# Scores before values in the entries of the stick-breaking attention units

## What is computed

```python
def stick_breaking(q, k, v, q_pos, k_pos):
    z = jnp.einsum('bqhd,bkhd->bhqk', q, k, ...) * (HEAD_DIM ** -0.5)
    earlier = k_pos[None, :] < q_pos[:, None]
    log_beta = jax.nn.log_sigmoid(z)
    log_keep = jnp.where(earlier, jax.nn.log_sigmoid(-z), 0.0)
    log_later = lax.cumsum(log_keep, axis=3, reverse=True) - log_keep
    weights = jnp.where(earlier, jnp.exp(log_beta + log_later), 0.0)
    return jnp.einsum('bhqk,bkhd->bqhd', weights.astype(v.dtype), v)
```

## Time and profile before

| what | value |
|---|---|
| median of three runs | 2002.44 us |
| profiled execution, its own time | 2002.01 us |
| its span on the core | 2000.3 us, granted TensorE clock 0.995 |
| TensorE busy | 1961.3 us (98%) |
| TensorE weight loads busy | 1790.4 us (90%) |
| VectorE busy | 1123.6 us (56%), 76% to 81% within the stretch of the stick-breaking units |
| ScalarE busy | 637.4 us (32%) |
| DMA | 285.31 MB, mean 143 GB/s |

### The profile page before, as it was taken

The page is one execution under the profiler, slowest core; times in us unless marked ns, Lnnn a source line. Parts: engine busy times, 40 slices in busy tenths (PEclk is TensorE's granted clock), DMA queues, the critical chain, the costliest instruction groups (busy, mean ns, idle before and its releaser), DMA issues.

```text
span 2000.3 us, 30761 instructions
## 1 busy us (share of the span) xinstructions
PE 1961.3 (98%) x12796; PEld 1790.4 (90%) x12796; DVE 1123.6 (56%) x2008; ACT 637.4 (32%) x1183; POOL 26.0 (1%) x73
## 2 busy tenths in 40 slices
PE   5999999999999999999999999999999999999998
PEld 5999999999999999899999999899999978877886
DVE  7368687776878676544445442654255563234234
ACT  7133333333333342222222221332133452232231
POOL 3000000000000000000000000000000000000000
PEclk9999999999999999999999999999999999999999
DMA  6457777776767767576665665554455553336523
GB/s 237 113 121 146 154 149 160 153 165 146 147 154 151 154 143 166 121 157 133 127 153 120 140 146 120 125 133 111 105 119 136 163 177 100 101 116 231 188 94 127
DMA packets 875749, 285.31 MB, mean 143 GB/s; under 512 B 617481, under 2 KB 850713, under 8 KB 873849
## 3 DMA queue, kind: packets, MB, share of 16 engines
q1 hardware_dynamic: 874440, 275.35, 58.1%
q0 software_dynamic: 1168, 7.99, 1.1%
HBM read 194.72 MB, written 91.75 MB: 143 GB/s over the span
## 4 chain that ended last, share of the span: by engine, by line
PE 93%; DVE 2%; DMA 2%; SPq 1%; ACT 0%; issue 0%; DVEq 0%; POOL 0%
PE ps L964 22%; PE ps L965 21%; PE ps L966 21%; PE ps L1176 5%; PE ps L1178 5%; PE ps L1177 5%; PE ps L1067 3%; PE ps L1146 3%; PE ps L1028 3%; PE ps L1117 3%; DMA arena<-in_x_prompt_dram 1%; DVE arena L1490 1%; DVE act_lo L1497 1%; DMA weight_scratch<-arena 1%; PE ps L1172 1%; PE ps L1173 1%
## 5 line engine op out<-in xcount | busy, mean ns | idle before, releaser
L964 PE MATMUL ps<-act_hi,w_hi 128*128 128x352 f32 x2688 | 879.0, 327 | 3.9 <-DVE arena L1529 3.9
L966 PE MATMUL ps<-act_hi,w_lo 128*128 128x352 f32 x2688 | 864.0, 321 | 0.0
L965 PE MATMUL ps<-act_lo,w_hi 128*128 128x352 f32 x2688 | 864.0, 321 | 0.0
L964 PEld LDWEIGHTS ps<-act_hi,w_hi 128*128 128x128 f32 x2688 | 505.5, 188 | 21.2 <-issue 18.2
L965 PEld LDWEIGHTS ps<-act_lo,w_hi 128*128 128x128 f32 x2688 | 506.6, 188 | 0.0
L966 PEld LDWEIGHTS ps<-act_hi,w_lo 128*128 128x128 f32 x2688 | 505.3, 188 | 0.0
L1505 DVE TENSOR_TENSOR w_lo<-w_raw,w_hi 128x512 fp32r<-128x512 f32 x348 | 236.0, 679 | 263.6 <-ACT w_hi L1350 209.5
L1277 ACT ACTIVATE w_hi<-w_raw 128x512 fp32r<-128x512 f32 x224 | 139.1, 623 | 342.4 <-DMA w_raw<-in_w_in_dram 342.0
L1176 PE MATMUL ps<-w_hi,act_hi 128*128 128x512 f32 x496 | 195.7, 395 | 2.0 <-DVE w_lo L1505 2.0
L1178 PE MATMUL ps<-w_hi,act_lo 128*128 128x512 f32 x496 | 194.6, 392 | 0.0
L1177 PE MATMUL ps<-w_lo,act_hi 128*128 128x512 f32 x496 | 194.5, 392 | 0.0
(11 more groups left out here) (137 smaller groups left out, 1502.1 us busy)
## 6 DMA issues: line engine op xcount, KB each, us to landing
w_raw<-in_w_in_dram SPq DMA_DIRECT2D x176, 256.0 KB, 3.4
w_raw<-in_w_out_dram SPq DMA_DIRECT2D x124, 256.0 KB, 2.6
weight_scratch<-arena SPq DMA_DIRECT2D x216, 128.0 KB, 3.4
arena<-weight_scratch SPq DMA_DIRECT2D x54, 512.0 KB, 4.4
w_raw<-in_w_in_dram SPq DMA_DIRECT2D x96, 128.0 KB, 3.1
weight_scratch<-arena SPq DMA_DIRECT2D x80, 132.0 KB, 4.0
arena<-weight_scratch SPq DMA_DIRECT2D x40, 256.0 KB, 3.4
arena<-in_x_prompt_dram SPq DMA_DIRECT2D x8, 1024.0 KB, 5.4
```

Of the source, the lines that this page charges most:

```text
L964: mm(bank(g, GN), wh, ah, start=(k == 0), stop=False)
L965: mm(bank(g, GN), wh, al, start=False, stop=False)
L966: last = mm(bank(g, GN), wl, ah, start=False, stop=(k == KT - 1))
```

## The change

`values_at` gives the values of a stick-breaking step another due time. For steps 0 to 5 of all six units, and for steps 6 to 8 of units 0 to 4, it is now the start of the pair that begins with the even step, plus 0.02 for an even step and plus 0.03 for an odd one, where it was 0.02 before the start. An entry then runs: scores n, scores n+1, masks of both, values of step n-4, values of step n-3.

```diff
     if kind == "a":
         if n + FLIGHT < STEPS["a"]:
-            return START[u][n + FLIGHT] - 0.02
+            return START[u][n + FLIGHT - (n + FLIGHT) % 2] + 0.02 + 0.01 * (n % 2)
         if n + 1 == STEPS["a"] and u < LAST_A:
             return START[u + 1][2] + 3.5
         if u < LAST_A:
-            return START[u + 1][n + FLIGHT - STEPS["a"]] - 0.02
+            return START[u + 1][n + FLIGHT - STEPS["a"] - (n + FLIGHT) % 2] + 0.02 + 0.01 * (n % 2)
         return chain_at(u, n) + 14.6
```

## The result

| | before | after |
|---|---|---|
| median of the runs | 2002.10 us (6 runs, 1998.81 to 2003.38) | 2011.38 us (6 runs, 2006.71 to 2014.06) |
| ratio, with its 95% interval | | 1.0049 (1.0035 to 1.0063) |
| profiled execution | 2002.01 us | 2006.71 us |
| its span, granted TensorE clock | 2000.3 us, 0.995 | 2005.0 us, 0.996 |

The changed kernel is slower by 9.3 us in the medians; 10.3 us had been forecast. Its profiled execution happens to be the fastest of its six, and shows only 4.7 us. So the comparison has two halves: what the six stick-breaking units lost, which the trace's records show to a tenth of a microsecond, and what happened behind them.

What follows compares the result with a forecast made beforehand. TensorE was taken to bound the kernel. Odd-score waits of 8.0 us plus 2.3 us for matmul shape changes gave 10.3 us on the profiled 2002.01, so 2012.3, and 2012.7 for the median; range 2006 to 2019.

Steps and rivals of the forecast that it cites:

- The bound: TensorE holds 93% of the last-ending chain and never waits inside the six units, so an earlier chain there buys nothing.
- The odd scores wait, steps 6 and 7, five units: In units 1 to 5, odd scores wait for VectorE's step 5 subtraction, 1.18 us each, 5.9 us together.
- It does not mend itself, because of the copy: VectorE waits 2.42 us, until 274.97, for TensorE's projection tile before step 5's turn, so step 5's end follows TensorE.
- The release: From the end of VectorE's operation to the first matmul waiting for it: 0.15 us, read at 817.57 us.
- Steps 8 and 9, units 1 to 5: no wait: The entry alone would wait 0.63 us, but TensorE is already 1.18 us later and VectorE follows only some 0.25.
- Unit 0: Odd-score waits of 1.33 us (steps 4, 5), 0.52 (steps 6, 7) and 0.27 (steps 8, 9), sum 2.1 us.
- Steps 4 and 5, unit entries: no wait: Units 1 to 5: at most 0.1 us at steps 4 and 5, taken as none; unit entries covered by 0.14 us.
- The change of shape in masked entries: 16 entries with masks pay one more matmul shape switch, 0.15 us each, 2.3 us; lower bound 0.8 us.
- Entries without masks swap like for like: In the 12 reordered entries without masks, the changes of matmul shape cost the same as before: zero.
- The clock: Rival: seven waits each bring a lower-clock stretch, 12 us more, 2024; chance 0.03 for all, 0.1 for a few.
- that the odd scores do not wait: Rival: no waits in the units, only the matmul shape cost of 0.8 to 2.3 us, 2003 to 2005; chance 0.12.
- That the 3.9 us wait swallows the loss: Rival, faster: TensorE's waits at 817.57 and near 1295 us swallow up to 6.4 us; 1997 us, chance 0.04.

Runs made afterwards that it cites:

- the repeat: The changed kernel run once more with no edit: 2011.35 us (5 runs), ratio 1.0049 to the kernel before.
- the control with the late copy: The kernel before, with one VectorE copy of a projection tile part per unit due 0.75 tick later: 2003.73 us (one run).

## Why the prediction held, and where it didn't

The forecast was 10.3 us (2012.7); the medians say 9.3 (2011.38) and, in the repeat, 10.4, the units alone 9.78 and 9.49. By its own steps:

- **The bound.** Right. Nothing on TensorE waited for the chain that now starts earlier, so only the added idle time and the shapes count. The prediction's "three real" waits are not the whole list; the kernel before also has 8.3 us for VectorE's L1497, in five waits before 49 us, and 2.0 us for L1505 at 1616 and 1823 us. All lie outside the units, so the argument stands.
- **The odd scores wait, steps 6 and 7, five units.** Forecast 1.18 us each; the entries grew by 1.186 to 1.189 by the records. The sum 5.9 is the main term, and the run of this entry alone (+6.58 us with unit 0's 0.54) bears it out. The listed idle time is 0.92, since records overlap.
- **It does not mend itself, because of the copy.** Right, and shown: with the copy moved the wait is gone.
- **The release.** I took 0.15 us from a copy on VectorE to the matmul. That row is a projection matmul, and there it is 0.15 us after the change too; before the scores it is 294.90 - 294.84 = 0.06 us. The missing part comes behind the start: the first record after the pause is longer (693 ns instead of 589, by the records), and the next follows later. Two errors that cancel, except in front of the sample's mask, where only the 0.05 us remain. That is why the sample's wait was 0.52 and not 0.63.
- **Steps 8 and 9, units 1 to 5: no wait.** Right, and the run of the sample entry alone shows it for the given reason: left without the loss in front of it, the wait stands there. The mix waits 0.28 us, as forecast (0.25). By the records step 7's subtraction ends 0.76 us after the entry's start in unit 1, where it was 1.53, so VectorE followed 0.4 of TensorE's 1.19 us, a little more than forecast, and the scores still came 0.25 us behind it. The single parts add to 6.58 + 2.37 + 2.39 us, with unit 0's entry of steps 4 and 5, taken from the changed kernel's profile, 1.5 more, 12.8 in all, where the whole change costs 9.8. The waits do not add.
- **Unit 0.** Forecast 1.33, 0.52 and 0.27 us. In the first profile its entries grew by 1.46, 0.54 and 0.26, that is waits of 1.33 and 0.54, and of 0.38 less the sample's 0.12. In the repeat the third wait was absent. That it came near the forecast in the first profile is luck: it hangs on the weight block described above, which the prediction had no term for. Unit 0 also has two waits at L1028, so "one per unit" was too few: the list shows seven there and one at L1034.
- **Steps 4 and 5, unit entries: no wait.** Right, in five units. By the records step 3's subtraction ends 0.42 us later against its entry in unit 1, between the "none" and the "all" of the forecast's 1 us.
- **The change of shape in masked entries.** Forecast 0.15 us x 16 = 2.3, the upper bound, taken by the nearest row; the product is 2.4, and the terms themselves give 0.14 x 16 = 2.2. Measured 0.14 x 16 = 2.2. From the start of the last mask to the first values, which no row had shown, 271.67 - (271.12 + 0.62 - 0.22) = 0.15 us pass. The rule from the Trainium skill, TensorEngine Tiling (Array Packing), Key Properties, is that a changed tiling mode drains the engine. The trace agrees as far as the cost goes: an entry with one change more costs more, 0.12 to 0.20 us, in all runs.
- **Entries without masks swap like for like.** This step failed for the sample entry. I said it would be "unchanged". Its last matmuls have the shape 128*64, as the values do. Values directly behind them need no change of shape, so the entry goes from four changes to three: in the first profile the first values record starts at 317.25, inside the last pair of the sample's scores. Six entries, 0.12 us each: 0.73 us less than forecast. This is the largest difference between the forecast 10.3 and the units' 9.78; small ones the other way (0.1 us in unit 0's third wait, the rest under 0.1 us each) make up the balance.
- **The clock.** Right: eight waits of 0.3 to 1.1 us, and the granted clock over the units stays 1.00.

The rivals: that the odd scores do not wait is refuted by the list of waits. That the 3.9 us wait swallows the loss is refuted by its unchanged 3.9 us. The DMA wait behind it did shrink from 2.5 to 1.5 us in the first profile, but was 2.3 us in the repeat, and 1.3 us where the units had lost nothing (even scores, values, sample scores). Of the clock rival nothing was seen inside the units; behind them the lower clock comes and goes with every order, and a stretch of 6.8 us at half the clock is worth 3.4 us. With the shorter DMA wait this is why the first profile showed half of the loss.

## What to carry to other kernels

Where one engine never waits, moving its work to the front can, apart from the seams, only expose waits: before doing so, ask for each operand and buffer of the moved work when its last reader ends, and for paired buffers ask it of the second of the pair, which here decided. Then look for the operation that ties the other engine to the busy one, since it decides whether a lost microsecond is regained later; moved by three quarters of a tick, one copy turned a loss of 9 to 10 us into one of 2 to 3. And count the changes of matmul shape by the shape of the first and last matmul at each seam, not by the name of the step.

## What the runs showed of the hardware that I had not expected

- A pause costs more than its idle time. After a wait for VectorE the first float32 score record took 693 ns instead of 589, and the interval to the next was 0.53 us instead of 0.42, though the shape had not changed: some 0.10 us, as much as one side of a change of shape. Before a bf16 mask record the same pause cost nothing beyond its idle time.
- A score or mask matmul starts 0.05 to 0.06 us after the end of the VectorE operation that released it, in all waits of the units. The projection matmul behind the 3.9 us wait starts 0.15 us after it, in every profile. Why they differ no run here shows.
- Between matmuls of one shape a different purpose shows no cost: from the sample's scores to the values, 6 ns lie between two starts.
- The 3.9 us wait at about 818 to 828 us brought a stretch at the lower clock in all ten profiles, of 3.4 us in seven and of 6.8 us in three; the later wait of 1.3 to 2.5 us for a DMA brought none, 3.4 or 6.8 us. Three windows from 1290 to 1310 us show it, of the kernels with steps 6 and 7 alone, the masked entries alone, and the sample entry alone (the granted clock is the third number from the end):

```profile
1290.00:1310.00 20.00, 17.86 (x120) 16.40 (x117) 9.14 (x32) 5.52 (x21) 0.00 (x0) 0.83 0.40 89
```

```profile
1290.00:1310.00 20.00, 17.56 (x140) 15.91 (x139) 7.69 (x29) 4.40 (x17) 0.00 (x0) 1.00 0.48 105
```

```profile
1290.00:1310.00 20.00, 17.93 (x134) 15.92 (x132) 6.69 (x22) 4.00 (x16) 0.00 (x0) 0.91 0.41 93
```

The waits for the DMA there were 2.1, 2.4 and 2.1 us: nearly the same wait, and three different clocks. What decides between them no run here shows; it is one part of the spread of this kernel's executions. Another lies in TensorE's waits for VectorE's L1505 (the low part of the weights) between 1611 and 1840 us: together they took from 1.1 us (changed kernel, first profile) to 4.7 us (the control with the late copy).
